# One subtraction of four 128x128 blocks instead of two of two blocks in a hybrid decoder's weight split

## The reference

```python
h = rmsnorm(x, norm_mix)
proj = h @ w_in            # q, k, v, g_ret, x_lru, y_lru, g_a, g_b
o, S_new = retention(rope(q), rope(k) * DK ** -0.5, v, S_ret)   # 4 heads, DK 256, DV 512
ret_branch = (silu(g_ret) * groupnorm(o) * gn_gain) @ w_ret_out
xc, new_buf = causal_conv(x_lru, conv_buf, conv_w, conv_b)      # width 1280, 4 taps
hl, h_last = rg_lru(xc, lru_wa, lru_ba, lru_wx, lru_bx, lru_lambda, h_lru)
lru_branch = (gelu(y_lru) * hl) @ w_lru_out
merged = sigmoid(g_a + b_gate[0]) * ret_branch + sigmoid(g_b + b_gate[1]) * lru_branch
x = x + merged @ w_o
gt, up = split(rmsnorm(x, norm_ffn) @ w_gate_up)                # 1024 -> 2 x 2816
x = x + (silu(gt) * up) @ w_down
```

## Time and profile before

| what | value |
|---|---|
| three runs | 2465.33, 2459.17, 2466.25 us (median 2465.33) |
| profiled execution | 2467.48 us, its span 2465.9 us |
| mean granted TensorE clock | 0.993 |
| busy: TensorE | 2408.1 us (98%), 19460 matmuls |
| busy: GpSimd | 1719.7 us (70%), 1970 instructions |
| busy: VectorE | 1200.5 us (49%) |
| busy: ScalarE | 630.5 us (26%) |
| low part, L380 | 1544 instructions, 1274.8 us |
| high part, L375 | 420 instructions, 442.3 us |

### The profile page before, as it was taken

How to read it: one execution, slowest core, us unless ns; L and a number is a source line. 1 busy time by engine, 2 the same in 40 slices (tenths; PEclk the granted TensorE clock), 3 DMA queues, 4 the chain that set the end, 5 groups by cost and what they waited for, 6 DMA issues and landing times.

```text
span 2465.9 us, 51507 instructions
## 1 busy us (share of the span) xinstructions
PE 2408.1 (98%) x19460; PEld 2353.5 (95%) x19460; DVE 1200.5 (49%) x1602; ACT 630.5 (26%) x913; POOL 1719.7 (70%) x1970
## 2 busy tenths in 40 slices
PE   7999999999999999999999999999999999999997
PEld 7898989999999999999998999999999999999997
DVE  7655555478853532022366455544886545221222
ACT  2312121227751211011113222222466412100110
POOL 7474747478887877777764747575898777777775
PEclk9999999999999999999999999999999999999999
DMA  5554545432233222222246636353222332223222
GB/s 174 180 183 155 168 154 169 159 97 82 86 94 85 95 94 86 93 94 88 89 131 208 206 118 221 122 200 105 89 91 84 96 91 93 89 86 98 94 82 89
DMA packets 120212, 296.94 MB, mean 120 GB/s; under 512 B 19136, under 2 KB 19648, under 8 KB 120064
## 3 DMA queue, kind: packets, MB, share of 16 engines
q1 hardware_dynamic: 60480, 198.21, 25.2%
q10 hardware_dynamic: 59584, 96.56, 11.7%
HBM read 254.34 MB, written 40.38 MB: 120 GB/s over the span
## 4 chain that ended last, share of the span: by engine, by line
PE 64%; DVE 2%; ACT 2%; DMA 1%; issue 1%; POOL 1%; DVEq 1%; ACTq 0%; POOLq 0%; SPq 0%
PE banks L394 61%; PE banks L568 1%; DMA w_raw<-in_wstream 1%; PE banks L530 1%; POOL w_low L380 1%; PE banks L584 1%; DVE scratch L933 1%; DMA scratch<-in_sret 0%; PE banks L560 0%; POOLq L376 0%; ACT scratch L1405 0%; PE banks L547 0%; ACT scratch L1404 0%; DVE ret_acc L1315 0%; DVE scratch L1040 0%
## 5 line engine op out<-in xcount | busy, mean ns | idle before, releaser
L380 POOL TENSOR_TENSOR w_low<-w_raw,w_high 128x256 fp32r<-128x256 f32 (+1 forms) x1544 | 1274.8, 856 | 61.8
L375 POOL TENSOR_SCALAR w_high<-w_raw 128x1024 fp32r<-128x1024 f32 (+3 forms) x420 | 442.3, 1053 | 663.1 <-PE banks L394 602.5
L394 PE MATMUL banks<-x_high,w_high 128*128 128x260 f32 x4096 | 835.3, 285 | 35.7 <-DVE x_low L747 11.1
L394 PE MATMUL banks<-x_high,w_low 128*128 128x260 f32 x4096 | 828.7, 284 | 2.3 <-issue 2.3
L394 PE MATMUL banks<-x_low,w_high 128*128 128x260 f32 x4096 | 827.2, 284 | 0.0
L394 PEld LDWEIGHTS banks<-x_high,w_high 128*128 128x128 f32 x4096 | 635.5, 190 | 48.9 <-issue 30.4
L394 PEld LDWEIGHTS banks<-x_high,w_low 128*128 128x128 f32 x4096 | 634.8, 189 | 0.0
L394 PEld LDWEIGHTS banks<-x_low,w_high 128*128 128x128 f32 x4096 | 634.2, 189 | 0.0
L394 PE MATMUL banks<-split_scratch,w_high 128*128 128x260 f32 x3776 | 607.8, 283 | 1.0 <-POOL w_low L380 0.8
L394 PEld LDWEIGHTS banks<-split_scratch,w_high 128*128 128x128 f32 x3776 | 516.9, 188 | 2.2 <-issue 1.2
L394 PE MATMUL banks<-split_scratch,w_low 128*128 128x260 f32 x1888 | 378.7, 282 | 0.0
(11 more groups left out here) (167 smaller groups left out, 1904.8 us busy)
## 6 DMA issues: line engine op xcount, KB each, us to landing
w_raw<-in_wstream SPq DMA_DIRECT2D x268, 512.0 KB, 3.5
w_raw<-in_wstream SPq DMA_DIRECT2D x88, 384.0 KB, 3.0
scratch<-in_sret ACTq DMA_DIRECT2D x64, 512.0 KB, 6.8
out_ret_s<-scratch ACTq DMA_DIRECT2D x64, 512.0 KB, 3.6
scratch<-v_rows ACTq DMA_DIRECT2D x64, 256.0 KB, 4.0
w_raw<-in_wstream SPq DMA_DIRECT2D x48, 320.0 KB, 2.8
w_raw<-in_wstream SPq DMA_DIRECT2D x16, 448.0 KB, 3.2
out_ret_p<-scratch ACTq DMA_DIRECT2D x8, 512.0 KB, 2.8
```

Of the source, the lines that this page charges most:

```text
L375: pool.tensor_scalar(WH[:, j, w], WR[:, j, w], 1.0, 0.0, ALU.mult, ALU.add)
L380: m = pool.tensor_tensor(WL[:, j, p], WR[:, j, p], WH[:, j, p].bitcast(F32), ALU.subtract)
L394: m = pe.matmul(out, wt[:, w, blk * P:(blk + 1) * P], x[xi], start=first and n == 0, stop=last and n == 2)
```

## The change

PIECE goes from 2 to 4. A half of four blocks is subtracted by one instruction of 128x512, a half of three blocks by one of 128x384; halves of two blocks or one are as before. The instructions of L380 go from 1544 to 840. The semaphores, the values waited for, the transfers and the other engines' programs stay.

```diff
-PIECE = 2
+PIECE = 4
```

## The result

The changed kernel takes 2478.98 us (median of six runs, 2476.71 to 2482.82) against 2465.79 us for the kernel before (six runs, 2459.17 to 2467.35). The ratio is 1.0054, with a 95% interval of 1.0044 to 1.0064: 13.2 us slower. The forecast was 2462.2 us, range 2456 to 2469; the time lies outside it, on the side that had a chance of 0.09. The profiled execution took 2482.82 us (span 2481.2 us, mean clock 0.992), 15.3 us of span more than the one before.

A forecast was written before the change was run, and what follows sets the result against it. The prediction took TensorE, busy 98%, as the bound, with GpSimd a supplier nearly always early. Gains of 4.6 us and losses of 1.5 us gave -3.1 us, so 2462.2 us from a median of 2465.3, range 2456 to 2469.

The forecast's parts named there:

- those 8.9 us: TensorE's waits for GpSimd's low part, 8 places: the most, with what they drag behind, that GpSimd savings could buy.
- The price of a 128x512: GpSimd's low part: one merged instruction takes about 1.24 us instead of 1.40, bounds 0.74 and 1.48 us.
- The hold on VectorE: Where VectorE and GpSimd alternate: a 128x512 holds VectorE 1.14 us instead of 0.60, up to 0.54 us longer.
- rival C: RG-LRU stage: VectorE becomes late, TensorE waits for L1114 once the chain is 0.28 us longer; 2471.5 us, chance 0.17.
- The gains: TensorE's shorter waits, earlier transfers and less half-clock time: 2.3 + 1.2 + 0.3 + 0.8 = 4.6 us.
- the six short waits: TensorE's short waits on GpSimd's low part, 2.6 us together: 2.3 us of them go.
- The two long ones: TensorE's waits of 3.50 and 2.83 us behind late transfers: each 0.6 us shorter, 1.2 us together.
- the fall of the clock behind them: Half-clock stretch after the long wait, 2.3 us lost: a third of it, 0.8 us, counted as gained.
- L865: VectorE's read after five contended L1040, for which TensorE waits: 0.2 us later in both layers, 0.4 us.
- L1053 behind the two L933: Tile read after two contended VectorE instructions: 0.54 us later reaches TensorE, 1.1 us over both layers.
- The replay: RG-LRU stretch, a unit of 6 blocks: L1085 ends 0.54 us later, but L1151 still ends at 623.11, level.
- C's worse case: RG-LRU stage: the following high part also slips in ahead of L1151, 1.16 x 8 = 9.3 us; chance of slower 0.09.

The follow-up runs named there:

- e10: Kernel before, with one instruction a half only in the 16 units of the merge stage: 2468.65 us, ratio 1.0013 to the kernel before.
- e1: Changed kernel, but two instructions a half in the 21 units of the RG-LRU stage's first channel group: 2470.89 us, ratio 1.0007 to the kernel before.
- e2: Kernel before, with one instruction a half only in the 21 units of the RG-LRU stage's first channel group: 2477.14 us, ratio 1.0035.
- e8c: Kernel before, GpSimd untouched, VectorE making four superfluous reads of each of a layer's first five gate tiles: 2480.82 us, ratio 1.0062.
- e9: Changed kernel with one of three convolution tap additions left out of VectorE's chain in later tiles: 2470.57 us, ratio 1.0004 to the kernel before.
- e7: Kernel before, with one instruction a half only from the first RG-LRU output projection unit to the merge stage's end: 2467.01 us, ratio 0.9993.
- e11: Changed kernel, but two instructions a half in the RG-LRU stage's first three units: 2472.72 us, ratio 1.0039 to the kernel before.
- c2: The kernel of e11 measured a second time: 2481.65 us, ratio 1.0046 to the kernel before.

## Why the prediction was wrong, point by point

**What bounds the kernel.** Right: TensorE is still busy for 97%, and most of what came off GpSimd became idle time. But "everything taken off it can buy TensorE no more than those 8.9 us" caps the gain alone; the loss had no such cap.

**The price of a 128x512.** Right: 1.24 us forecast, 1.285 us alone, median 1.292 over all forms. "420 of them" was a slip: the second half of a unit of 8 is four blocks too, so 688 are 128x512. The busy time fell by 174 us, not 113, most likely because fewer turns with VectorE also mean fewer waits inside GpSimd's records.

**The hold on VectorE.** Right for one meeting: 1.14 us forecast, and L1151 at 1.62 us where it was 1.06 is +0.56 (0.54 forecast). The Trainium skill's rule (SBUF — State Buffer, section Who interferes with whom), which the prediction set behind rival C, is borne out by these rows.

**The gains.** Of the 2.6 us of the six short waits one of 0.3 us is left: 2.3, as forecast. The two long ones fell by 3.6 us together in the first execution of the changed kernel and by 1.2 in the second (2.89 and 2.27 us), where 1.2 was forecast; the fall of the clock behind them is in neither. TensorE comes to the first of them some 9 to 10 us later than before, so part of this may be the loss upstream being given back. e10, which leaves the upstream alone, shortened the first by 1.4 us and not the second. The gains were not over-sized.

**The losses that were counted.** L865: 3.9 to 4.3 us, +0.4 in two places, as forecast. L1053 behind the two L933: forecast +0.5 each; the waits vanished there (0.66 and 0.69 us before, none at 496.07 and 1715.84), where the two L933 of layer 1 take 3.26 us instead of 3.75: fewer turns, not a longer hold. The 3.7 us on L1053 after are another place, the entry.

**The step that failed: rival C, and what was set against it.** The mechanism was named, with the wait on L1114 as its sign, and given 0.17 at 2471.5 us; in the sum of the forecast the RG-LRU stage stood at nothing, where the runs have 13.3 us more waiting on its three reads. Two readings made it too small.
(1) "In the stretch of rows 6 ... level." The replay took one stretch of a unit of 6 blocks, where one lump replaces two pieces. Over a whole round there are two units of 8 and two of 6, and VectorE meets lumps at L1122, L1136, L1146, L1078 and L1151 and a copy at L1085: +2.4 us, not 0. And the replay kept the unit beside L1085 and L1151, while in the round the quicker GpSimd had moved on by one: the copy of the next unit (608.59, eight blocks) now holds L1085, 1.36 us, and its first 128x512 (610.32) holds L1151, 1.62 us. A high part slipping in was the condition of C's worse case, and it is what happens. L1130, forecast at 1.6 us, is the one that meets nothing there (0.70).
(2) "It decides as soon as the chain is longer by 0.28 us." The matmul at 624.98 was taken to wait for the L1114 that ends at 624.70. With a ring of four slots its slot had been free since long before; the nearness of the two rows was chance. The slot that is needed next is the one that L1162 gives back. In the kernel before, L1162 and the first matmul of the x tile that takes its slot:

```profile
603.02 0.70 DVE L1162 TENSOR_TENSOR scratch<-banks,rinv 128x520 f32<-128x520 f32 x1
...
606.25 0.41 PE L394 MATMUL banks<-x_high,w_high 128*128 128x260 f32 x2
```

(VectorE's and TensorE's rows of one timeline.) L1162 ends at 603.72, so it is 2.5 us early. After, L1162 ends at 613.22 and TensorE starts at 613.27. From round to round even that is not the margin, since L1162 also releases the next round's L1122 through ScalarE: the loop has 1.5 us to spare, and a chain longer by 2.4 us makes a round longer by 0.9 once the 2.5 us are used up. Two of layer 0's four rounds are 21.1 us for 20.2, with waits on L1162 that read 0.70 and 0.71 us, less than the 0.92 lost; the others are 20.8 and 20.5. The six waits are 0.26 to 0.71 us in layer 0, 0.17 and 2.23 in layer 1, whose rounds are less even. The two errors pulled apart: by the margin alone C should have looked certain, by the replay harmless. I believed the replay.

**What no step had.** The entry (1.84 us a layer, at 547 and at 1767 us, with a half-clock stretch behind the first alone) and the second group's start (L1114, 1.35 to 1.7 us in two places a layer). The prediction looked for places where TensorE already waits, and for one where it nearly did; these had their margins in other rows. Entry, rounds and second group together are 14.7 us of waits on the three lines, less the 1.4 that L1053 had before: 13.3. Against them stand 5.8 us less waiting for GpSimd and 6.1 us more of TensorE's busy time, half-clock stretches among it, where the span grew by 15.3. That the first sum comes near the 13.2 us measured is therefore no proof; e1, e2, e8c and e9 are what shows the cause.

## What to carry to other kernels

Where two engines hold each other for whole instructions, the length of an instruction on the one with time to spare is a cost on the other, even if its busy time falls: look for a chain on the other engine that frees something, and sum it over a whole round of the loop. Take the margin from the wait that the consumer really has (which slot, which read), not from two rows that stand near each other, and look for a loop that carries one round's lateness into the next. A constant for the size of a piece can be set by stage, but here even the best setting (e7) was level with the middle value.

## What the runs showed of the hardware that was not expected

- Even a tiny instruction is held until the other engine's ends: L1136, 128x8, took 0.43 us beside pieces of 128x256 and 0.98 us beside 128x512, ending at 596.94 where GpSimd's two 128x512 end at 596.92.
- VectorE's L1151 takes 0.70 us where it meets nothing (at 660.92), 1.06 us against pieces of 128x256 and 1.62 against one of 128x512; GpSimd's two 128x512 beside it take 3.24 us, where three 128x256 took 3.30.
- Half-clock stretches of 3.4 us (18 matmuls for 31), or twice that, sometimes follow a wait of TensorE and sometimes don't: after 1.84 us at 547.37 the clock was 0.50, after 1.84 us at 1767.14 and 1.70 us at 676.65 it stayed at 1.00. Up to the last matmuls the profiled executions of all these kernels hold four to nine of them (one of 6.8 us counted as two), at 1.6 us each; two executions of one kernel had 8 and 7 (the changed one), or 5 and 7 (e11, c2). What sets them off was not tried.
